# An attention stage laid on a list of half slots, in a one-core encoder layer

## The reference, cut to what matters

```python
dq = rope(rms_norm(dq.reshape(B, L, 16, 64), qnorm_g), pos)      # and dk alike
s = einsum('bqhcd,bkhcd->bhcqk', q, k) * 64 ** -0.5              # c: the two maps
p = softmax(where(visible, s, -1e30), axis=-1)
a = p[:, :, 0] - lam * p[:, :, 1]
o = rms_norm(einsum('bhqk,bkhv->bqhv', a, v), subln_g) * (1 - lam_init)
merged = sigmoid(g_ret) * (ret_o @ w_br_ret) + sigmoid(g_diff) * (o @ w_br_diff)
```

## Time and profile before

| | |
|---|---|
| median of 3 runs | 1671.64 us (1670.87 to 1671.95) |
| the profiled execution | 1673.31 us, of which its instructions span 1671.5 us |
| PE busy | 1519.2 us, 91% |
| DVE, ACT, POOL busy | 835.2 us (50%), 650.3 us (39%), 356.9 us (21%) |
| mean granted clock of PE | 0.96 |

### The profile page before, as it was taken

How to read it: one execution, slowest core, us unless ns; L and a number is a source line. 1 busy time by engine, 2 the same in 40 slices (tenths; PEclk the granted TensorE clock), 3 DMA queues, 4 the chain that set the end, 5 groups by cost and what they waited for, 6 DMA issues and landing times.

```text
span 1671.5 us, 21282 instructions
## 1 busy us (share of the span) xinstructions
PE 1519.2 (91%) x7820; PEld 1141.5 (68%) x7820; DVE 835.2 (50%) x1418; ACT 650.3 (39%) x1066; POOL 356.9 (21%) x197
## 2 busy tenths in 40 slices
PE   4999999999999999997998788889989699999991
...
GB/s 342 127 89 139 149 177 74 130 152 195 56 126 192 159 76 129 162 76 148 96 114 38 51 138 133 70 64 154 255 166 51 142 338 363 395 390 390 383 318 201
DMA packets 158091, 290.31 MB, mean 174 GB/s; under 512 B 15083, under 2 KB 40859, under 8 KB 157733
## 3 DMA queue, kind: packets, MB, share of 16 engines
...
## 4 chain that ended last, share of the span: by engine, by line
PE 29%; DVE 10%; DMA 8%; ACT 3%; issue 3%; SPq 1%; POOL 0%; DVEq 0%; ACTq 0%; POOLq 0%
PE pj L93 7%; PE pj L95 7%; PE pj L94 7%; DMA m_raw<-w 6%; DVE d_tmp L2163 1%; DVE d_sm L2174 1%; ACT d_E L1958 1%; PE d_B L2440 1%; DMA ring_raw<-w_out 1%; PE d_B L2467 1%; PE d_B L2459 1%; PE d_B L2501 1%; ACT m_hi L1377 1%; PE d_B L1552 1%; PE d_B L2478 1%
## 5 line engine op out<-in xcount | busy, mean ns | idle before, releaser
L93 PE MATMUL pj<-ring_hi,hT_hi 128*128 128x512 f32 x880 | 371.3, 422 | 20.5 <-ACT d_q_rows L1938 9.9
L95 PE MATMUL pj<-ring_hi,hT_lo 128*128 128x512 f32 x880 | 349.6, 397 | 0.0
L94 PE MATMUL pj<-ring_lo,hT_hi 128*128 128x512 f32 x880 | 349.0, 397 | 0.0
L479 POOL TENSOR_TENSOR ring_lo<-ring_raw,ring_hi 128x1024 fp32r<-128x1024 f32 x79 | 191.9, 2430 | 552.8 <-ACT ring_hi L545 552.8
L545 ACT ACTIVATE ring_hi<-ring_raw 128x1024 fp32r<-128x1024 f32 x79 | 83.4, 1058 | 424.5 <-DMA ring_raw<-w_in 358.9
L1456 DVE TENSOR_TENSOR m_lo<-m_raw,m_hi 128x1024 fp32r<-128x1024 f32 x188 | 223.9, 1221 | 25.6 <-ACT m_hi L1377 23.2
L93 PEld LDWEIGHTS pj<-ring_hi,hT_hi 128*128 128x128 f32 x880 | 168.8, 192 | 80.2 <-issue 34.6
L1377 ACT ACTIVATE m_hi<-m_raw 128x1024 fp32r<-128x1024 f32 x188 | 194.7, 1058 | 28.8 <-DMA m_raw<-w 25.1
L95 PEld LDWEIGHTS pj<-ring_hi,hT_lo 128*128 128x128 f32 x880 | 168.4, 191 | 38.0
L94 PEld LDWEIGHTS pj<-ring_lo,hT_hi 128*128 128x128 f32 x880 | 169.2, 192 | 30.6 <-issue 1.0
L1903 POOL TENSOR_TENSOR ring_lo<-ring_raw,ring_hi 128x1024 fp32r<-128x1024 f32 x37 | 89.7, 2424 | 362.4 <-ACT ring_hi L1923 362.4
...
...
## 6 DMA issues: line engine op xcount, KB each, us to landing
m_raw<-w SPq DMA_DIRECT2D x188, 512.0 KB, 10.8
...
```

The costliest lines, as they stand in the source:

```text
L93: pe.matmul(out, s_hi, m_hi, start=start, stop=False)
L94: pe.matmul(out, s_hi, m_lo, start=False, stop=False)
L95: return pe.matmul(out, s_lo, m_hi, start=False, stop=stop)
L479: pool.tensor_tensor(lo[:, p], raw[:, p], hi[:, p].bitcast(F32), ALU.subtract).then_inc(lo_done, 1)
```

## The change

The list is written in half slots, one step each, so that `attend` stands ahead of every step; events that are bound to a projection's slots (`place`) happen at even half slots. In it:

- Half 0 keeps a unit in 4 half slots; half 1 gets a unit in 3, where it had 2, and begins at 194 (slot 97). Turn and values stand 6 and 8 half slots behind the scores in both. On PE the scores come first in a half slot, map 1 ahead of map 0; maximum and exponential are done map by map. The reduction writes the negated maximum, and the scale of the scores is multiplied into the table of the queries' gains. Map 1's exponential alternates between `E[:, 2]` and a part of `vc`, so `vc` is loaded only behind the last unit of a half.
- `take_rows` only copies. `square_rows` squares the copies one by one in the half slots behind, and `head_squares` follows tile by tile; root and rotations stand 4 or 5 slots further on. The turns of half 0 stand later (7 slots for the queries' first), those of half 1's keys up to 4 slots earlier.
- In a sample, exponential, scaling, turn and values stand further behind the scores (s_turned 9 and s_valued 17 half slots behind the keys, where 6 and 14 stood). The norm of half 0's output moves to the units of half 1 (`O_NORM`).
- GD0 is taken by a plain copy; its sigmoid is done in place in BR0.
- SP asks for a piece after the caches of the same half slot. POOL's `block_q(1)` moves from GD1's pieces to GD0's.

```diff
-SLOTS = 20
+STEPS = KT * NT
+BETWEEN = -2
 UNITS = NP_T * 4
+O_NORM = 205, 211, 217, 223, 229
...
+def place(h):
+    return DIFF_GROUPS[h // STEPS], h % STEPS // 2 if h % 2 == 0 else BETWEEN
...
-        self.first, self.step, self.lag = ((42, 2, 3), (102, 1, 2))[i]
-        self.cache = (76, 120)[i]
-        self.turns = ((10, 12, 14, 16, 18), (79, 81, 85, 89, 93))[i], ((30, 32, 34, 36, 38), (96, 97, 98, 99, 100))[i]
-        self.out = ((123, 125, 129, 133, 137), (140, 141, 142, 143, 149))[i]
+        self.first, self.period = ((84, 4), (194, 3))[i]
+        self.cache = (152, 246)[i]
+        self.turns = ((34, 38, 42, 46, 50), (158, 162, 170, 178, 186))[i], ((64, 68, 72, 76, 80), (188, 190, 192, 196, 198))[i]
+        self.out = ((248, 252, 256, 264, 272), (280, 282, 284, 286, 302))[i]
...
+    def unit(self, h, after):
+        u = h - self.first - after
+        return u // self.period if u >= 0 and u % self.period == 0 and u // self.period < UNITS else None
+
+    def scored(self, h):
+        return self.unit(h, 0)
...
+    def combined(self, h):
+        return self.unit(h, 2)
...
+    def turned(self, h):
+        return self.unit(h, 6)
...
+    def valued(self, h):
+        return self.unit(h, 8)
...
+    def keys_turned(self, h):
+        return self.stream(h, 0)
+
+    def s_scored(self, h):
+        return self.stream(h, 3)
+
+    def s_turned(self, h):
+        return self.stream(h, 9)
+
+    def s_valued(self, h):
+        return self.stream(h, 17, 8, DEC_B // 2)
...
+    def rows_squared(self, h, a):
+        t = h - STEPS * RING_GROUPS.index(("K0", "V0", "K1", "V1")[2 * self.i + a]) - 2
+        return t // 2 if 0 <= t < 2 * NT and t % 2 == 0 else None
...
+        def exp_of(u, m):
+            return E[:, u % 2] if m == 0 else E[:, 2] if u % 2 == 0 else vc[:, 1, 0]
...
                     job_done(sp, "V", i, j - 1)
-                elif i:
-                    job_done(sp, "V", 0, DEC_B // 2 - 1)
...
-            load_vc(0, 0)
...
-                if m % 5 == 4 and (name != "BR1" or m < 10):
-                    load_piece(RING_GROUPS[group(name) + 1], m // 5)
+            for s in range(STEPS * len(DIFF_GROUPS)):
...
                 for half in halves:
                     i = half.i
                     b = half.keys_turned(s)
                     if some(b) and (b + 1 < DEC_B or i == 0):
                         load_kc(*((i, b + 1) if b + 1 < DEC_B else (1, 0)))
                     j = half.s_valued(s)
-                    if some(j) and (j + 1 < DEC_B // 2 or i == 0):
-                        load_vc(*((i, j + 1) if j + 1 < DEC_B // 2 else (1, 0)))
+                    if some(j) and j + 1 < DEC_B // 2:
+                        load_vc(i, j + 1)
+                    if half.combined(s) == U - 1:
+                        sp.wait_ge(A_done, (i + 1) * U)
+                        load_vc(i, 0)
...
+                if s % 10 == 9 and (name != "BR1" or s % STEPS < 20):
+                    load_piece(RING_GROUPS[group(name) + 1], s % STEPS // 10)
...
+                    if p == 1 and name in ("Q1", "GD0"):
                         pool.wait_ge(lo_done, n + 1)
-                        block_q(int(name == "GD1"))
+                        block_q(int(name == "GD0"))
...
             def take_rows(i, a):
-                n = norm_index(i, a)
                 if i and a:
                     act.wait_ge(krow_out, 32)
                 for t in range(NT):
-                    job = n * NT + t
                     if (i, a) != (0, 0):
                         bank_done(act, "QK"[a] + str(i), t)
-                    if job >= 2:
-                        act.wait_ge(reduced, job - 1)
-                    if n and t < 2:
-                        act.wait_ge(roped, n * NT)
-                    act.activation(tmp[:, t % 2], pj[t][:], ACT.Square).then_inc(squared, 1)
                     act.activation(rows[a][:, t], pj[t][:], ACT.Copy).then_inc(pj_free[t], 1)
+
+            def square_rows(i, a, t):
+                job = norm_index(i, a) * NT + t
+                bank_taken(act, "QK"[a] + str(i), t)
+                if job >= 2:
+                    act.wait_ge(reduced, job - 1)
+                if t < 2 and job >= NT:
+                    act.wait_ge(roped, job - t)
+                act.activation(tmp[:, t % 2], rows[a][:, t], ACT.Square).then_inc(squared, 1)
...
-            def exps(i, u):
+            def exps(i, u, m):
                 nk, n = unit_of(u)[2], i * U + u
-                act.wait_ge(nmax_done, n + 1)
-                if u >= 2:
+                act.wait_ge(nmax_done, 2 * n + 2 - m)
+                if m == 0 and u >= 2:
                     job_done(act, "A", i, u - 2)
-                if n >= 1:
-                    act.wait_ge(A_done, n)
-                for m in range(2):
-                    act.activation(E[:, u % 2 if m == 0 else 2, 0:nk], job_bank("S", i, u, m)[:, 0:nk], ACT.Exp, scale=SCALE,
-                                   bias=sm[:, u % 4, 2 + m:3 + m], accum_out=sm[:, u % 4, 4 + m:5 + m]).then_inc(job_free("S", i, u, m), 1)
+                if m == 1 and n >= 2:
+                    act.wait_ge(A_done, n - 1)
+                act.activation(exp_of(u, m)[:, 0:nk], job_bank("S", i, u, m)[:, 0:nk], ACT.Exp,
+                               bias=sm[:, u % 4, 2 + m:3 + m], accum_out=sm[:, u % 4, 4 + m:5 + m]).then_inc(job_free("S", i, u, m), 1)
...
-                act.activation(Ps[:], job_bank("C", i, b)[:, 0:KEYS], ACT.Exp, scale=SCALE, bias=sms[:, 1:2],
+                act.activation(Ps[:], job_bank("C", i, b)[:, 0:KEYS], ACT.Exp, bias=sms[:, 1:2],
...
-                    elif name in ("GD1", "BR0"):
-                        j = int(name == "BR0")
-                        take(f"GD{j}", lambda t: sg[:, t, j * W:(j + 1) * W], ACT.Sigmoid)
+                    elif name == "GD1":
+                        take("GD0", lambda t: sg[:, t, 0:W], ACT.Copy)
+                    elif name == "BR0":
+                        take("GD1", lambda t: sg[:, t, W:], ACT.Sigmoid)
+                if name == "BR0" and 6 <= m < 6 + NT:
+                    bank_taken(act, "GD0", m - 6)
+                    act.activation(sg[:, m - 6, 0:W], sg[:, m - 6, 0:W], ACT.Sigmoid).then_inc(gate_done, 1)
...
+                        if some(half.rows_squared(s, a)):
+                            square_rows(i, a, half.rows_squared(s, a))
...
-                    if some(half.valued(s - 1)):
-                        n = half.valued(s - 1)
-                        square_o(i, n, o[i][:, n // HH, n % HH * P:(n % HH + 1) * P])
-                    if some(half.s_valued(s - 1)):
-                        j = half.s_valued(s - 1)
-                        square_o(i, U + j, o[i][:, NP_T, j * P:(j + 1) * P])
                     if some(half.turned(s)):
                         take_A(i, half.turned(s))
                     if some(half.scored(s)):
-                        exps(i, half.scored(s))
+                        for a in (1, 0):
+                            exps(i, half.scored(s), a)
+                    if some(half.valued(s - 3)):
+                        n = half.valued(s - 3)
+                        square_o(i, n, o[i][:, n // HH, n % HH * P:(n % HH + 1) * P])
+                    if some(half.s_valued(s - 2)):
+                        j = half.s_valued(s - 2)
+                        square_o(i, U + j, o[i][:, NP_T, j * P:(j + 1) * P])
...
-                    if some(half.s_scored(s)):
-                        s_exp(i, half.s_scored(s))
+                    if some(half.s_scored(s - 2)):
+                        s_exp(i, half.s_scored(s - 2))
...
+                do(dve.tensor_scalar(gains[:, 0], gains[:, 0], SCALE, None, ALU.mult))
...
+            def head_squares(i, a, t):
+                job = norm_index(i, a) * NT + t
+                dve.wait_ge(squared, job + 1)
+                ins = dve.tensor_reduce(st[:, 0, t * 8:(t + 1) * 8], tmp[:, t % 2].rearrange("p (g c) -> p g c", c=DDH), AX, ALU.add)
+                ins.then_inc(reduced, 1)
+                if t == NT - 1:
+                    dve.wait_ge(reduced, job + 1)
+                    do(dve.tensor_scalar(st[:, 1], st[:, 0], 1.0 / DDH, EPS, ALU.mult, ALU.add))
...
-            def maxima(i, u):
-                nk, c = unit_of(u)[2], sm[:, u % 4]
-                for m in range(2):
-                    job_done(dve, "S", i, u, m)
-                    links(dve.tensor_reduce(c[:, m:m + 1], job_bank("S", i, u, m)[:, 0:nk], AX, ALU.max))
-                links.sync()
-                dve.tensor_scalar(c[:, 2:4], c[:, 0:2], -SCALE, None, ALU.mult).then_inc(nmax_done, 1)
+            def maximum(i, u, m):
+                job_done(dve, "S", i, u, m)
+                dve.tensor_reduce(sm[:, u % 4, 2 + m:3 + m], job_bank("S", i, u, m)[:, 0:unit_of(u)[2]], AX, ALU.max, negate=True) \
+                   .then_inc(nmax_done, 1)
...
             def combine(i, u):
                 nk, c = unit_of(u)[2], sm[:, u % 4]
-                for m in range(2):
```

(65 more changed lines are left out.)

103 lines of the change are left out of this document (37 added, 66 removed).

## The result

The changed kernel takes 1634.89 us (median of 4 runs, 1634.28 to 1636.23) where the one before takes 1671.80 in the same runs (1670.87 to 1672.42): a ratio of 0.9779, interval 0.9763 to 0.9795. The profiled execution took 1634.28 us with a span of 1632.5 and a mean granted clock of 0.969; against 1673.31 and 1671.5 that is 39.0 us less, where the prediction's sum has 41.7.

A forecast was written before the change was run, and what follows sets the result against it. PE bound by order, not throughput, from K0 to BR0 (422.3 us, floor 356.4). Pauses 49.1 to 17.7 (-31.4), first wait -0.5, clock -9.8: -41.7 from 1673.31 gives 1631.6, 1629.9 for a median run; said 1630, range 1616 to 1653.

The forecast's parts named there:

- K0, -6.0: Start of K0: with rows copied first nothing waits, so PE's 6.0 us pause goes.
- The 2 us kept for a dip at the start: Start of K0: a short dip to the lower clock stays, 2 us kept where its busy part had cost 3.8.
- The later rotations don't hold PE: K0 on: later rotations cost PE nothing, as the first turn moves from slot 10 to half slot 34.
- K1 5 us, loop 6.1: K1: DVE's loop, reciprocal to reciprocal, falls from 7.17 to 6.1 us; K1 keeps 5 of 15.0 us of pause.
- V1 4, GD0 2, GD1's inner 1.2: Pauses left: V1 4 of 11.4 us, GD0 2 of 9.1, GD1 1.2 of 3.5.
- 2.3 us ahead of GD1 and 1.7 ahead of BR0: Starts of GD1 and BR0: new PE pauses of 2.3 and 1.7 us, both waiting for ACT.
- `acc` 0.5 of 0 to 1.5: BR0: acc's 2.5 MB ahead of BR1's first piece may stop ACT at its split, 0 to 1.5 us, 0.5 taken.
- The wait for a cache, 2.1: Samples' turned keys: with the cache asked for ahead of the piece, the one 2.1 us wait goes.
- The clock: K0 to BR0: cost of the lower clock falls from 16.8 to 7 us, -9.8; 14 us spent there, not 41.
- B: K0 to BR0: DVE's loop hardly shortens, K1 keeps 12, V1 10, GD0 7 us; about 1652 us, chance 0.14.
- C: Turns of cached keys: the single cache buffer becomes the bound; slower, 1692 us if transfers land at 9; chance 0.04.
- D: Behind BR0: the gain turns up as a wait where transfers are the bound; about 1671 us, chance 0.05.

The follow-up runs named there:

- e1: The changed kernel with squares taken from the bank ahead of the copies again, in K0, V0, K1 and V1: 1645.61 us, ratio 0.9852.
- e2: The kernel before the change, with only take_rows altered to copy the banks first and then square the copies: 1673.38 us, ratio 1.0013.
- e5: The changed kernel with half 1's units begun two half slots earlier, from 192 instead of 194: 1635.91 us, ratio 0.9783.
- e7: The changed kernel with both maxima, then a third small instruction that the exponentials wait for, as before: 1645.79 us, ratio 0.9854.
- e9: The changed kernel with half 0's keys turned later, at half slots 68 to 97 instead of 64 to 80: 1633.49 us, ratio 0.9766.
- e14: The changed kernel with K1's root one slot later, behind the unit's combination, and its rotations two slots later: 1634.71 us, ratio 0.9796.
- e3: The changed kernel with half 1's units every 2 half slots from 204, at the old distances of 4 and 6: 1652.50 us, ratio 0.9888.
- e13: The changed kernel with half 1's turn and values 4 and 6 half slots behind the scores, units still every 3 from 194: 1637.29 us, ratio 0.9802.
- after: The changed kernel itself, with the whole change against the kernel before: 1634.89 us, ratio 0.9779.
- e4: The changed kernel with the reload of acc in BR0 asked for behind BR1's first piece: 1630.07 us, ratio 0.9756.
- e6: The changed kernel with SP asking for the weight piece ahead of the caches in a half slot: 1640.24 us, ratio 0.9826.

## Why the prediction was right

It was right in the time and in most of its mechanism, and wrong in two of its steps (V0 and `acc`). By its own steps, in their order; the four numbers that matter are pauses 22.8 (predicted 17.7), clock 5.0 (7), the floor 382.0 - 22.8 - 5.0 = 354.2 (356.4), and the stretch -40.3 (-41.2 and -0.5 at its start). Why the floor is 2.2 us lower, with the same matmuls, no run shows.

- *K0, -6.0.* Right: no pause in it at all. That the copies first do this is shown by e1, that they would do nothing in the old list by e2; the second the prediction did not say. The first wait is 2.46 us, predicted 2.2. The 2 us kept for a dip at the start were wrong for this execution and right for others: in the traces of e5, e7, e9 and e14, whose work in K0 is the same, K0 has a dip and is 1.6 longer.
- *"The later rotations don't hold PE"*, and with it V0 and Q1 at 1 us. This step failed. V0 has 4.9 us of pause and a dip. DVE is busy 34.75 of 38.26 us there, because seven rotations, the tail of an eighth and the root meet POOL's pieces, and the turns of keys at half slots 64 to 80 wait for them. The longest of these waits, 2.38 us, is for a rotation behind a root of which POOL held one instruction for 2.28 us instead of 0.20. The prediction saw when the first turn of queries comes, and did not lay DVE's queue out up to the last turn of keys.
- *K1 5 us, loop 6.1.* The loop was right: 6.53 us as measured, of which 0.46 is PE at the lower clock, so 6.07, and 5.98 in the next period without POOL's hold. So was the 0.8 us for the early exponential and the small instruction, which come out at 0.9 (e7). K1 has 6.7 us of pause instead of 5. The terms that were too small are the root and POOL's pieces, 3 us in the sum: 4.4 us are the root's place and POOL's hold on it (e14), 1.9 POOL's hold on a rotation.
- *V1 4, GD0 2, GD1's inner 1.2.* Measured 2.5, 1.5 and 0.5. The unit in 3 half slots, with its earlier start, is worth some 15 us (e3 against e13). The feared waits of `s_values` for a bank, 1.6 us, don't appear.
- *2.3 us ahead of GD1 and 1.7 ahead of BR0.* Right in place and cause, 1.9 and 1.4 us. These are the rows of after, PE's first step of GD1, and then ACT's at both borders:

```profile
1061.45 0.47 PE L93 MATMUL pj<-ring_hi,hT_hi 128*128 128x512 f32 x1 [1.91 <-ACT d_sg L1961]
```

```profile
1060.04 0.69 ACT L1975 ACTIVATE d_E<-d_B,d_sm 128x512 f32<-128x512 f32 x1
...
1060.70 2.55 ACT L1961 ACTIVATE d_sg<-pj 128x512 f32<-128x512 f32 x5
...
1121.44 1.28 ACT L1961 ACT_TABLE_LOAD   x1
1122.74 2.56 ACT L1961 ACTIVATE d_sg<-pj 128x512 f32<-128x512 f32 x5
```

  The copy of GD0 starts behind the second exponential, and the first sigmoid of GD1 0.02 us behind the table load. The profile puts the second wait down to issue; PE's step at 1123.43 follows the end of that first sigmoid. The page "ScalarE: Activation LUTs" of the Trainium skill (What ACT_TABLE_LOAD costs) counts a drain to a switch, by which the prediction worked out 3.1 us as an estimate; the trace has no room for one, with 0.02 us ahead of the load and 0.02 us behind it.
- *`acc` 0.5 of 0 to 1.5.* Mis-sized: 2.9 us and a dip, 4.5 in all (e4). The price was bounded by how long ACT might wait at its split, and not by where the piece stands behind 2.5 MB. The five sigmoids in place, priced at nothing, are in it too: three of them stand between the late split and the last output.
- *The wait for a cache, 2.1.* 0.7 us are left, but the order is worth more than the wait it removed: with the new, tighter list the old order costs 5.4 us of waits and two dips (e6).
- *The clock.* Three dips in the stretch, 10.2 us, predicted 14 with the one at the start.

The misses are of both signs: V0 with Q1 +3.9, BR0 +2.9 and K1 +1.7 of pause, against V1 -1.5, GD0 -0.5, GD1's inner part -0.7 and the two borders -0.4 and -0.3, so +5.1 in all; the clock gives -2.0 and the floor -2.2, which leaves the stretch 0.9 us over the sum. That 1630 came so near 1634.9 is in part this balance. Of the rivals, B (K1 keeps 12, V1 10, GD0 7) didn't come about, nor C: the turns of cached keys wait 0.7 us in all for their transfers. D is refuted by the 472.24 us behind BR0. What e1, e3, e6 and e7 lose, one part undone at a time, sums to 44.5 us, more than the 36.9 there are, so these are not shares that add up. And no run undoes the longer distances in a sample, GD0's plain copy, the moved norms or the earlier `block_q`: that the samples' wait of 8.1 us is gone is seen in the trace, but by which of them is argued and not shown.
